# The w2 slabs of the expert stage, begun by ScalarE in a queue of its own

## The chip, the core and the metric

The kernel runs on one core of a Trainium2 chip. The metric is the device time of one launch in microseconds (us). The time before is the median of three runs.

## The reference, cut to what matters

The network has two blocks; the second has two layers, and each of these ends in a mixture of experts. 256 tokens of width 1024 are routed, each to the best two of eight experts in the best of four groups. Each of the 32 experts has three matrices of 2 MB in float32: w1 and w3 (1024 x 512) and w2 (512 x 1024).

```
def expert_block(args):
    tok_b, w_b, e = args
    xb = t[tok_b]
    hid = jax.nn.silu(xb @ w1[e]) * (xb @ w3[e])
    return (hid @ w2[e]) * w_b[:, None].astype(t.dtype)
```

## The kernel before, in words

The program is written out by hand for each engine, with semaphores in between. An expert stage (`moe0`, `moe1`) works through 16 pairs of experts, numbered 0 to 15, 64 token places for each expert. TensorE (`moe_pe`) runs this for pair i: `inner(i, "exp_w1")`, `inner(i, "exp_w3")`, some transposes and the gather of pair i + 1's tokens, and `outer(i)`, which multiplies by w2. After outer(i) comes inner(i + 1, "exp_w1"). Each `inner` or `outer` takes two slabs, one for each expert of the pair, and waits until both have landed. After the inner of pairs 3, 7 and 11 with w1 a few products for the next group of experts come in between; in pairs 4, 8 and 12 a scatter stands ahead of outer.

All weights come through eleven places of 2 MB in SBUF, taken in turn (`Places`, named ring, arena and XTGB in the trace). Slab n takes the place of slab n - 11 and must wait until TensorE has used that one (`free`). SyncE (`moe_sp`) begins every slab, in the order in which TensorE uses them: w1, w1, w3, w3, w2, w2 of pair 0, then of pair 1, and so on. One queue holds them all, so they also land in that order. The slabs of w3 and w2 of pair 15 come in halves.

ScalarE (`moe_act`) applies silu to what w1 gave, copies the transposed hidden values (`x_ht`), and then writes the gathered tokens of pair i + 1 (`turned_x`, eight ACTIVATE of 128x128). Those eight are done when outer(i) has just begun.

Of the kernel before, what the change touches and what calls it, by code (L numbers as in the profile page):

```python
# [12 lines left out]
P = 128  # L13
# [4 lines left out]
SLAB = 4096  # L18
# [6 lines left out]
class Board:  # L25
# [14 lines left out]
    def at(self, *key):  # L40
        if self.counting:
            return []
        return self.known[key]
# [139 lines left out]
def build(nc, d, out, consts):  # L183
    with ExitStack() as ctx:
        board = Board()
        at = board.at
# [32 lines left out]
        sems = {}  # L219
        for name in ("x0", "x1", "aq0", "aq1", "aq2", "aq3", "ident", "rope", "consts", "c", "pos", "gb", "sink", "maska", "ssmp", "late", "keep", "half0", "half1", "half2", "half3", "ada_b", "cols", "mod", "gate_b",  # L220
                     "fox_fb", "mla_g", "abias", "router_b", "rw", "dmask", "srow", "se0", "se1", "se2", "out"):
            sems[name] = ctx.enter_context(nc.semaphore("s_" + name))
        for i in range(NRING + 7):
            sems[f"ring{i}"] = ctx.enter_context(nc.semaphore(f"s_ring{i}"))
        for e in ("pe", "act", "dve", "pool"):
            for st in STAGES:
# [4 lines left out]
        for l in range(2):  # L231
            for j in range(3):
# [5 lines left out]
        ring = Places(slots + [None, None, XTGB] + [arena.ap[:, TOP + j * SLAB:TOP + (j + 1) * SLAB] for j in range(3)]  # L238
                      + [arena.ap[:, 0:SLAB]])
        ring.begin(NRING)  # L240
        shape = {}

        def load(sp, key, src, kc, n, hold=False):
            i, was = ring.take(key, hold)
# [29 lines left out]
        def load_behind_halves(sp, keys, name, offs, kc, n):  # L274

            place = {}
            for h in range(2):
                for key, off in zip(keys, offs):
                    if h == 0:
                        place[key] = ring.take(key)  # L280
                        shape[key] = (kc, n)
                    i, was = place[key]
                    sp.wait_ge(at("free" if h else "free half", was))
                    f = slice(h * SLAB // 2, (h + 1) * SLAB // 2)
                    src = d[name][off:off + P * SLAB].rearrange("(p f) -> p f", p=P)
                    sp.landed(sp.e.dma_start(ring.bufs[i][:, f], src[:, f]), f"ring{i}", ("w", key))
# [1559 lines left out]
        NP = NE // 2  # L1846
# [675 lines left out]
        def mix_dve(v, l, nn):  # L2522
# [11 lines left out]
            k = None  # L2534
            v.wait_ge(at("rope2"))
            for t in range(2):
                if t:
                    x_sums(v, l, nn)
                    for part in range(3):
                        slab_sums(v, l, 0, part)  # L2540
                v.wait_ge(at("rqk", l, t), k)
                k = rope(v, ps_of("rqk", l, t).rearrange("p (h x) -> p h x", h=8), 8, ctab[:, t * 64:t * 64 + 64],
                         stab[:, t * 64:t * 64 + 64], [rqk[:, t, :].rearrange("p (h x) -> p h x", h=8)], rtmp,
                         [("read", "rqk", l, t)], [("rqk rope", l, t)])
# [13 lines left out]
            slab_results(v, l, 1, 2)  # L2558
            slab_sums(v, l, 2, 2)
            slab_results(v, l, 1, 3)  # L2560
            v.wait_ge(at("dmask", l))
            for h in range(4):
                v.wait_ge(at("rs", l, h))
                if h >= 2:
# [7 lines left out]
            for q in range(8):  # L2572
                k = v.then_inc(v.e.bn_stats(st8[:, q, :], ps_of("ro", l, q // 4)[:, (q % 4) * P:(q % 4 + 1) * P]))
                v.wait_ge(k)
                k = v.then_inc(v.e.bn_aggr(mv8[:, q, :], st8[:, q, :]))
# [3 lines left out]
            for t in range(2):  # L2579
                for h in range(4):  # L2580
                    q = t * 4 + h
                    k = v.then_inc(v.ts(rqk[:, t, h * P:(h + 1) * P], ps_of("ro", l, t)[:, h * P:(h + 1) * P],
                                        mv8[:, q, 0:1], rs8[:, q:q + 1], ALU.subtract, ALU.mult), ("read", "ro", l, t))
# [18 lines left out]
            k = v.then_inc(v.tt(lf, misc[:, :, 0:4], fbb.unsqueeze(1).to_broadcast([P, 2, 4]), ALU.add))  # L2602
            v.wait_ge(k)
            k = v.then_inc(v.ts(lt_, lf, -1.0, None, ALU.mult))
# [39 lines left out]
            k = None  # L2644
            for t in range(2):
                kv = kpt[:, t, :].rearrange("p (c x) -> p c x", c=2)
                v.wait_ge(k)
                k = rope(v, misc[:, t, 388:452].unsqueeze(1), 1, ctab[:, t * 64:t * 64 + 64],
                         stab[:, t * 64:t * 64 + 64], [kv[:, 0:1, :], kv[:, 1:2, :]], mtmp, [], [("kp rope", l, t)])
            for t in range(2):  # L2650
                v.wait_ge(at("qp", l, t), k)
                k = rope(v, ps_of("qp", l, t)[:, 0:T].rearrange("p (h x) -> p h x", h=4), 4, ctab[:, t * 64:t * 64 + 64],
                         stab[:, t * 64:t * 64 + 64], [qpt[:, t, :].rearrange("p (h x) -> p h x", h=4)], mtmp,
                         [("read", "qp", l, t)], [])
                v.wait_ge(k)
                k = v.then_inc(v.ts(qpt[:, t, :], qpt[:, t, :], MS, None, ALU.mult), ("qp rope", l, t))
# [40 lines left out]
            k = v.then_inc(v.stt(g, g, 1.0, rgain[:, l, :], ALU.add, ALU.mult))  # L2697
# [294 lines left out]
        def moe_sp(sp, l):  # L2992
            for j, until in ((5, "gate row"), (2, "router")):
                ring.tenant[NRING + j] = (until, l)
                ring.turn.append(NRING + j)
            ring.turn.append(NRING + 6)
            for i in range(NP):
                if i == 2:
                    reg = flag_reg(sp, l)
                offs = [(l * NE + 2 * i + j) * P * SLAB for j in range(2)]  # L3000
                for k, nm in enumerate(("exp_w1", "exp_w3", "exp_w2")):
                    keys = [(nm, l, i, j) for j in range(2)]
                    kc, n = ((8, 512), (8, 512), (4, 1024))[k]
                    if all(ring.tenant[s] in HALVED[l] for s in ring.turn[0:2]):
                        load_behind_halves(sp, keys, nm, offs, kc, n)
                    elif k and i == NP - 1:
                        slabs_in_halves(sp, keys, nm, offs, kc, n, k == 1, 2 * (k == 1))
                    else:
                        for key, off in zip(keys, offs):
                            if key == ("exp_w1", l, 0, 0):  # L3010
                                continue
                            if ring.tenant[ring.turn[0]] in HALVED[l]:
                                load_behind_halves(sp, [key], nm, [off], kc, n)
                            else:
                                slab(sp, key, nm, off, kc, n)
            general(sp, l, reg, general_sp)
            last_over_gate[l] = ring.tenant[NRING + 5]
            last_over_mask[l] = ring.tenant[NRING + 6]
            ring.turn = [i for i in ring.turn if i < NRING]
# [211 lines left out]

        def moe_act(act, l, nn):
            act.stage(f"moe{l}")
            def turned_x(i):
                for c0 in (0, 4) if i else (0, 2, 4, 6):
                    act.wait_ge(at("xg", l, i, c0))
                    if i >= 1:
                        act.wait_ge(at("exp_w3", l, i - 1))
                    for c in range(c0, c0 + (4 if i else 2)):
                        ins = act.act(xg[:, c, :], ps_of("xg", l, i, c0)[:, (c - c0) * P:(c - c0 + 1) * P],  # L3240
                                      ACT.Identity, scale=mcol[l][:, 4, c:c + 1], bias=mcol[l][:, 3, c:c + 1])
                    act.then_inc(ins, ("xg ready", l, i, c0), ("read", "xg", l, i, c0))

            def group_rows(g):
                for n in range(2):
                    act.wait_ge(at("xr", l, g, n))
                    if g:
                        act.wait_ge(at("xg", l, 4 * g - 1, 4))
                    act.then_inc(act.cp(xr_q[:, :, n * 64:(n + 1) * 64],
                                        ps_of("xr", l, g, n).rearrange("p (q c) -> p c q", c=8)), ("xr ready", l, g, n),  # L3250
                                 ("read", "xr", l, g, n))

            group_rows(0)
            turned_x(0)
            act.wait_ge(at("ex", l))
            act.then_inc(act.act(ex, ex, ACT.Exp), ("exp ex", l))
            for i in range(NP):
                act.wait_ge(at("exp_w1", l, i))
                if i >= 1:
                    act.wait_ge(at("xht", l, i - 1))  # L3260
                act.then_inc(act.act(x_s, ps_of("exp_w1", l, i), ACT.Silu), ("silu", l, i),
                             ("read", "exp_w1", l, i))
                if i % 4 == 3 and i + 1 < NP:
                    group_rows(i // 4 + 1)
                act.wait_ge(at("xht", l, i))
                if i >= 1:
                    act.wait_ge(at("xy", l, i - 1, 1))
                act.then_inc(act.cp(x_ht, ps_of("xht", l, i).rearrange("p (a b) -> p a b", a=4)),
                             ("xht ready", l, i), ("read", "xht", l, i))
                if i + 1 < NP:  # L3270
                    turned_x(i + 1)
                if i == 1:
                    reg = flag_reg(act, l)
            general(act, l, reg, general_act)
            if l == 0:
                square_act(act, nn, 0, hrows, X, *av_done(l, 0))
                rms_rows(act, nn, 0, hrows, X, 4, 8)
                square_act(act, nn, 1, hrows, X, *av_done(l, 1))
                for t in range(2):
                    rms_turned_act(act, 1, nn, t)  # L3280
# [460 lines left out]
```

## Time and profile before

| | us |
|---|---|
| median of 3 runs (2283.49 to 2285.26) | 2283.55 |
| the profiled execution, its own time | 2283.03 |
| its span in the profile | 2281.2 |
| TensorE busy | 2249.4 |
| VectorE busy | 1057.5 |
| ScalarE busy | 461.1 |

The profile shows one execution. Busy time is the union of an engine's instructions; a wait stands in square brackets behind the instruction that ended it, with what released it. The span begins with the first instruction and ends with the last. The expert stages lie at about 1100 to 1545 us and 1830 to 2275 us.

### The profile page before, as it was taken

To read this page: it belongs to the slowest core of one execution; us is meant where nothing else is said; L and a number is where in the kernel's file an instruction comes from. 1 tells how busy PE (TensorE), PEld (TensorE's weight loads), DVE (VectorE), ACT (ScalarE), POOL (GpSimd) and SP (SyncE) were. 2 spreads that over 40 slices of the span, in tenths; PEclk is the share of its full clock that TensorE was granted. 3 is DMA by queue.
4 is the path that set the end of the run, shared out by engine and by line. 5 is a ranking of instruction groups with operands and counts; after the bars stand their busy time and mean duration, and the time that the engine had idled before them with its cause. 6 is when DMAs were issued, how large, how long until landed. Compare 5 with 4: busy or idle time off the path is not lost.

```text
span 2281.2 us, 26770 instructions
## 1 busy us (share of the span) xinstructions
PE 2249.4 (99%) x11302; PEld 1377.5 (60%) x11302; DVE 1057.5 (46%) x2098; ACT 461.1 (20%) x1041; POOL 74.4 (3%) x131
## 2 busy tenths in 40 slices
PE   9999999999999999999999999999999999999998
PEld 6569547886497459997533433335999743333343
DVE  4578756668588567675311111125767421111122
ACT  3411003358111011230211111101122021111111
POOL 2000000010000000000000000000000000000000
PEclk9999999999999999999999999999999999999999
DMA  7378725354689515246999999995424899999997
GB/s 296 116 313 358 309 76 202 149 184 162 246 346 407 181 54 211 98 185 256 410 427 428 428 427 427 427 419 210 175 78 168 344 426 427 427 427 428 427 427 285
DMA packets 59318, 672.52 MB, mean 295 GB/s; under 512 B 7521, under 2 KB 7809, under 8 KB 18865
## 3 DMA queue, kind: packets, MB, share of 16 engines
q1 hardware_dynamic: 51888, 649.45, 69.2%
q0 software_dynamic: 7296, 21.21, 2.7%
q8 instruction: 93, 1.52, 0.3%
q14 instruction: 41, 0.33, 0.0%
HBM read 667.37 MB, written 3.26 MB: 294 GB/s over the span
## 4 chain that ended last, share of the span: by engine, by line
PE 89%; DMA 7%; DVE 3%; issue 0%; POOL 0%; ACT 0%; SPq 0%; DVEq 0%; POOLq 0%; ACTq 0%
PE ps L101 86%; DMA ring<-in_exp_w 5%; DVE arena L114 1%; DVE arena L117 1%; PE ps L350 1%; DMA arena<-ssm_rows 1%; PE ps L3112 1%; DMA ring<-in_ada_w 0%; PE ps L639 0%; DMA ring<-in_attn_w_in 0%; PE ps L2139 0%; DVE X L117 0%; DVE arena L110 0%; PE ps L1328 0%; POOL small L117 0%
## 5 line engine op out<-in xcount | busy, mean ns | idle before, releaser
L101 PE MATMUL ps<-arena 128*64 128x512 f32 (+5 forms) x4612 | 1075.9, 446 | 12.6 <-DVE arena L117 4.6
L101 PEld LDWEIGHTS ps<-arena 128*128 128x128 f32 (+2 forms) x4612 | 536.5, 168 | 425.3 <-issue 393.5
L101 PE MATMUL ps<-ring,arena 128*64 128x512 f32 (+2 forms) x1592 | 501.8, 583 | 1.5 <-DMA ring<-in_exp_w 1.5
L101 PE MATMUL ps<-XTGB,ring 128*128 128x256 f32 (+1 forms) x2032 | 382.5, 344 | 0.0
L101 PEld LDWEIGHTS ps<-XTGB,ring 128*128 128x128 f32 x2032 | 333.5, 191 | 43.8 <-issue 9.5
L101 PEld LDWEIGHTS ps<-ring,arena 128*64 128x64 f32 (+1 forms) x1592 | 185.0, 151 | 240.7 <-issue 236.4
L122 DVE COPY arena<-ps 128x512 f32<-128x512 f32 (+5 forms) x133 | 63.3, 496 | 401.1 <-PE ps L101 282.3
L121 ACT COPY arena<-ps 128x512 f32<-128x512 f32 (+3 forms) x187 | 85.0, 473 | 690.2 <-PE ps L101 283.6
L117 DVE TENSOR_TENSOR arena<-ps,arena 128x256 f32<-128x256 f32 (+5 forms) x290 | 127.1, 475 | 119.1 <-PE ps L101 89.0
L101 PE MATMUL ps<-XTGB,arena 128*128 128x128 f32 (+2 forms) x736 | 178.4, 396 | 0.0
L101 PE MATMUL ps<-ring,XTGB 128*128 128x512 f32 (+3 forms) x484 | 166.4, 498 | 1.9 <-DMA ring<-in_attn_w_in 1.8
L117 DVE TENSOR_TENSOR arena<-arena,ps 128x512 f32<-128x512 f32 x36 | 24.7, 687 | 291.7 <-PE ps L101 291.7
L105 ACT ACTIVATE arena<-ps 128x512 f32<-128x512 f32 (+2 forms) x83 | 44.2, 536 | 554.8 <-PE ps L101 549.9
L105 ACT ACTIVATE arena<-arena 128x256 f32<-128x256 f32 (+4 forms) x235 | 119.3, 549 | 146.8 <-DVE arena L117 113.5
L117 DVE TENSOR_TENSOR arena<-arena 128x256 f32<-128x256 f32 (+7 forms) x272 | 127.2, 489 | 21.3 <-PE ps L101 11.0
L101 PEld LDWEIGHTS ps<-ring,XTGB 128*128 128x128 f32 x484 | 89.0, 191 | 70.8 <-issue 61.5
L101 PE MATMUL ps<-arena,ring 128*128 128x128 f32 (+1 forms) x960 | 131.3, 289 | 0.0
L101 PEld LDWEIGHTS ps<-arena,ring 128*128 128x128 f32 x960 | 122.2, 192 | 3.2
L101 PEld LDWEIGHTS ps<-XTGB,arena 128*128 128x128 f32 (+1 forms) x736 | 94.9, 173 | 39.7 <-issue 37.7
L114 DVE SCALAR_TENSOR_TENSOR arena<-arena 128x256 f32<-128x256 f32 (+3 forms) x224 | 94.2, 442 | 50.7 <-ACT arena L105 23.2
L114 DVE SCALAR_TENSOR_TENSOR arena<-ring,small,arena 128x512 f32<-128x512 f32 x140 | 105.3, 752 | 5.0
L105 ACT ACTIVATE arena<-ps,small 128x128 f32<-128x128 f32 (+1 forms) x264 | 96.8, 471 | 37.8 <-PE ps L101 37.7
(162 smaller groups left out, 1050.6 us busy)
## 6 DMA issues: line engine op xcount, KB each, us to landing
arena<-in_exp_w SPq DMA_DIRECT2D x96, 2048.0 KB, 28.9
ring<-in_exp_w SPq DMA_DIRECT2D x64, 2048.0 KB, 28.0
ring<-in_mlp_w SPq DMA_DIRECT2D x25, 2048.0 KB, 11.4
ring<-in_ada_w SPq DMA_DIRECT2D x20, 2048.0 KB, 9.5
XTGB<-in_exp_w SPq DMA_DIRECT2D x16, 2048.0 KB, 28.5
ring<-in_ssm_w_in SPq DMA_DIRECT2D x12, 2048.0 KB, 8.2
ring<-in_w_in SPq DMA_DIRECT2D x12, 2048.0 KB, 8.0
ring<-in_gate_w SPq DMA_DIRECT2D x12, 2048.0 KB, 7.9
```

Source lines behind the costliest of these rows:

```text
L101: return self.e.matmul(o, lhsT=lhsT, rhs=rhs, start=start, stop=stop, skip_group_check=True)
L105: return self.e.activation(o, i, func, bias=bias, scale=scale)
L114: return self.e.scalar_tensor_tensor(out=o, in0=i0, scalar=s, in1=i1, op0=op0, op1=op1)
L117: return self.e.tensor_tensor(o, a, b, op)
L121: return self.e.copy(o, i)
L122: return self.e.tensor_copy(o, i)
L350: ins = pe.e.transpose(ps[:, j * P:(j + 1) * P], i, C["ident"][0:m, 0:m])
L3112: ins = pe.e.transpose(ps[:, f * P:(f + 1) * P], x_h[:, f:512:4], C["ident"])
```

## The change

ScalarE begins the w2 slabs of pairs 2 to 13, in both expert stages: 12 pairs, two slabs each, two stages, 48 transfers. SyncE only books their places, so that every slab keeps the place that it had. ScalarE begins the two slabs of pair i + 1 in its turn i, right behind `turned_x(i + 1)`. They have semaphores of their own. Pairs 0, 1, 14 and 15 stay as they were. One wait is added on VectorE in the mixer, for a constant that landed much earlier.

```diff
--- before.py
+++ after.py
@@ -221,6 +221,7 @@
                      "fox_fb", "mla_g", "abias", "router_b", "rw", "dmask", "srow", "se0", "se1", "se2", "out"):
             sems[name] = ctx.enter_context(nc.semaphore("s_" + name))
         for i in range(NRING + 7):
+            sems[f"ringa{i}"] = ctx.enter_context(nc.semaphore(f"s_ringa{i}"))
             sems[f"ring{i}"] = ctx.enter_context(nc.semaphore(f"s_ring{i}"))
         for e in ("pe", "act", "dve", "pool"):
             for st in STAGES:
@@ -238,7 +239,7 @@
         ring = Places(slots + [None, None, XTGB] + [arena.ap[:, TOP + j * SLAB:TOP + (j + 1) * SLAB] for j in range(3)]
                       + [arena.ap[:, 0:SLAB]])
         ring.begin(NRING)
-        shape = {}
+        shape, place_of = {}, {}
 
         def load(sp, key, src, kc, n, hold=False):
             i, was = ring.take(key, hold)
@@ -2558,7 +2559,7 @@
             slab_results(v, l, 1, 2)
             slab_sums(v, l, 2, 2)
             slab_results(v, l, 1, 3)
-            v.wait_ge(at("dmask", l))
+            v.wait_ge(at("late"), at("dmask", l))
             for h in range(4):
                 v.wait_ge(at("rs", l, h))
                 if h >= 2:
@@ -3003,6 +3004,10 @@
                     kc, n = ((8, 512), (8, 512), (4, 1024))[k]
                     if all(ring.tenant[s] in HALVED[l] for s in ring.turn[0:2]):
                         load_behind_halves(sp, keys, nm, offs, kc, n)
+                    elif k == 2 and 2 <= i < NP - 2:
+                        for key, off in zip(keys, offs):
+                            place_of[key] = (*ring.take(key), off)
+                            shape[key] = (kc, n)
                     elif k and i == NP - 1:
                         slabs_in_halves(sp, keys, nm, offs, kc, n, k == 1, 2 * (k == 1))
                     else:
@@ -3231,6 +3236,15 @@
 
         def moe_act(act, l, nn):
             act.stage(f"moe{l}")
+
+            def load_w2(i):
+                for j in range(2):
+                    key = ("exp_w2", l, i, j)
+                    s, was, off = place_of[key]
+                    act.wait_ge(at("free", was))
+                    act.landed(act.e.dma_start(ring.bufs[s], d["exp_w2"][off:off + P * SLAB].rearrange("(p f) -> p f", p=P)),
+                               f"ringa{s}", ("w", key))
+
             def turned_x(i):
                 for c0 in (0, 4) if i else (0, 2, 4, 6):
                     act.wait_ge(at("xg", l, i, c0))
@@ -3269,6 +3283,8 @@
                              ("xht ready", l, i), ("read", "xht", l, i))
                 if i + 1 < NP:
                     turned_x(i + 1)
+                if 2 <= i + 1 < NP - 2:
+                    load_w2(i + 1)
                 if i == 1:
                     reg = flag_reg(act, l)
             general(act, l, reg, general_act)
```

On SyncE, the end of an expert stage before: the slabs of pairs 12, 13 and 14, each row one matrix of a pair or a part of one (`in_exp_w1` is expert matrix w1).

```order
L248 DMA arena<-in_exp_w1 128x4096 x2
L248 DMA arena<-in_exp_w3 128x4096 x2
L248 DMA XTGB<-in_exp_w2 128x4096
L248 DMA arena<-in_exp_w2 128x4096
L248 DMA ring<-in_exp_w1 128x4096 x2
L248 DMA ring<-in_exp_w3 128x4096 x2
L248 DMA arena<-in_exp_w2 128x4096 x2
L248 DMA arena<-in_exp_w1 128x4096 x2
L248 DMA arena<-in_exp_w3 128x4096
L248 DMA XTGB<-in_exp_w3 128x4096
L248 DMA arena<-in_exp_w2 128x4096
L248 DMA ring<-in_exp_w2 128x4096
```

The same place in the changed program:

```order
L249 DMA arena<-in_exp_w1 128x4096 x2
L249 DMA arena<-in_exp_w3 128x4096 x2
L249 DMA ring<-in_exp_w1 128x4096 x2
L249 DMA ring<-in_exp_w3 128x4096 x2
L249 DMA arena<-in_exp_w1 128x4096 x2
L249 DMA arena<-in_exp_w3 128x4096
L249 DMA XTGB<-in_exp_w3 128x4096
L249 DMA arena<-in_exp_w2 128x4096
L249 DMA ring<-in_exp_w2 128x4096
```

The w2 rows of pairs 12 and 13 have left SyncE's queue; those of pair 14 are still there.

On ScalarE before, around its turn 12: the tokens of pair 13 (two rows of four ACTIVATE), then silu and the copy of the hidden values of pair 13, then the tokens of pair 14.

```order
L105 ACTIVATE arena<-ps0,small 128x128 x4
L105 ACTIVATE arena<-ps1,small 128x128 x4
L105 ACTIVATE arena<-ps3 128x512
L121 COPY arena<-ps0 128x512
L105 ACTIVATE arena<-ps1,small 128x128 x4
L105 ACTIVATE arena<-ps7,small 128x128 x4
```

The same place in the changed program:

```order
L105 ACTIVATE arena<-ps0,small 128x128 x4
L105 ACTIVATE arena<-ps1,small 128x128 x4
L3245 DMA arena<-in_exp_w2 128x4096 x2
L105 ACTIVATE arena<-ps3 128x512
L121 COPY arena<-ps0 128x512
L105 ACTIVATE arena<-ps1,small 128x128 x4
L105 ACTIVATE arena<-ps7,small 128x128 x4
```

The two transfers of pair 13's w2 now stand behind the tokens of pair 13 and ahead of its silu.

## Rows read from the trace of the kernel before

**Rows 1.** The page: busy time of the engines, DMA share in 40 slices.

```profile
PE 2249.4 (99%) x11302; PEld 1377.5 (60%) x11302; DVE 1057.5 (46%) x2098; ACT 461.1 (20%) x1041; POOL 74.4 (3%) x131
...
DMA  7378725354689515246999999995424899999997
```

**Rows 2.** Stretches: length, busy time of each engine, granted clock, DMA share, GB/s.

```profile
1184.00:1435.00 251.00, 250.03 (x1163) 98.88 (x1159) 36.93 (x79) 40.93 (x97) 0.00 (x0) 1.00 1.01 427
1435.00:1465.00 30.00, 29.13 (x131) 11.85 (x131) 6.89 (x12) 3.84 (x10) 0.00 (x0) 1.00 1.01 428
```

**Rows 3.** TensorE's timeline, first stage: start, us, instruction, wait before it.

```profile
1408.63 7.09 PE L101 MATMUL ps<-ring,arena 128*64 128x512 f32 x32
...
1435.84 8.14 PE L101 MATMUL ps<-arena 128*64 128x512 f32 x34 [1.82 <-DMA arena<-in_exp_w]
...
1465.20 1.08 PE L101 MATMUL ps<-ring,arena 128*64 128x512 f32 x4 [0.23 <-DMA ring<-in_exp_w]
...
1484.74 0.65 PE L101 MATMUL ps<-arena 128*64 128x512 f32 x2 [0.75 <-issue]
```

**Rows 4.** Chain that ended last, first stage: start, us, what.

```profile
1354.34 8.07 PE ps L101 x34
...
1390.84 25.94 PE ps L101 x110
...
1427.20 37.87 DMA ring<-in_exp_w
```

**Rows 5.** TensorE's timeline, the same four places of the second stage.

```profile
2163.35 1.08 PE L101 MATMUL ps<-arena 128*64 128x512 f32 x4 [1.76 <-DMA arena<-in_exp_w]
...
2192.71 0.65 PE L101 MATMUL ps<-ring,arena 128*64 128x512 f32 x2 [0.23 <-DMA ring<-in_exp_w]
...
2212.24 0.65 PE L101 MATMUL ps<-arena 128*64 128x512 f32 x2 [0.74 <-issue]
...
2242.93 1.51 PE L101 MATMUL ps<-ring,arena 128*64 128x512 f32 x6 [1.03 <-DMA ring<-in_exp_w]
```

**Rows 6.** ScalarE's timeline, first stage.

```profile
1335.69 2.91 ACT L105 ACTIVATE arena<-ps,small 128x128 f32<-128x128 f32 x8 [1.17 <-PE ps L101]
...
1364.76 2.91 ACT L105 ACTIVATE arena<-ps,small 128x128 f32<-128x128 f32 x8 [1.17 <-PE ps L101]
1379.65 0.60 ACT L105 ACTIVATE arena<-ps 128x512 f32<-128x512 f32 x1 [11.99 <-PE ps L101]
...
1389.87 2.90 ACT L105 ACTIVATE arena<-ps,small 128x128 f32<-128x128 f32 x8 [1.17 <-PE ps L101]
...
1419.18 2.90 ACT L105 ACTIVATE arena<-ps,small 128x128 f32<-128x128 f32 x8 [1.17 <-PE ps L101]
...
1446.32 2.91 ACT L105 ACTIVATE arena<-ps,small 128x128 f32<-128x128 f32 x8 [1.17 <-PE ps L101]
```

**Rows 7.** DMA queues at 1101 to 1113: packets, MB, share of 16 engines.

```profile
q1 hardware_dynamic: 265, 3.98, 78.0%
q0 software_dynamic: 250, 1.02, 20.9%
```

**Rows 8.** Single transfers: out_w, then the expert slabs begun at 1442 to 1444.

```profile
DMA to landing us min/median/max: 7.7/10.1/12.4
...
L248 SPq DMA_DIRECT2D arena<-in_exp_w x2: 328/380/433, 1443.0 to 1443.3; - x2
...
DMA to landing us min/median/max: 41.7/43.9/46.2
```

**Rows 9.** SyncE's timeline: the slabs begun there.

```profile
1442.96 0.80 SPq L248 DMA_DIRECT2D arena<-in_exp_w  x2
...
1523.59 4.92 SPq L248 DMA_DIRECT2D ring<-in_w_in  x4
```

**Rows 10.** TensorE's longest wait, and the stretch behind it (columns of rows 2).

```profile
1548.63 1.86 PE L350 MATMUL ps<-c_ident,arena 128*128 128x128 f32 x8 [4.09 <-issue]
...
1549.00:1552.00 3.00, 2.87 (x9) 1.93 (x9) 1.43 (x5) 1.51 (x4) 0.00 (x0) 0.50 0.69 295
```

## The prediction

> **What bounds the kernel now.** I read the page first. TensorE is busy for 99% of the span, and the DMA engines are at nine tenths in two long blocks, the expert stages [rows 1]. Then the stretches: from 1184 to 1435 us TensorE is busy for 250 of 251 us at the full granted clock (1.00, the 2.4 GHz level), and the DMA engines are at 1.01 of their time with 427 GB/s [rows 2]. Both limits bind. Which ends last is told by TensorE's own waits. In the first stage it waits 1.82 us for w3 of pair 12, 0.23 for w3 of pair 13 and 0.75 for w1 of pair 14 [rows 3], 2.8 us in all; in the second 1.76, 0.23, 0.74 and 1.03 for w1 of pair 15 [rows 5], 3.8 in all. So both stages start with weights well ahead; the transfers lose ground pair by pair, because a pair's six slabs need 6 x 4.9 = 29.4 us and TensorE's pair needs about 25 to 29; and the two meet at pair 12. The chain says the same: 37.87 us from begin to landing at 1427.20 + 37.87 = 1465.07, the one long DMA piece of this stage [rows 4].
>
> One number rests on this: the slab period. W3 of pair 12 landed at 1435.84 - 0.14 = 1435.70 (0.14 being what lies between the landing at 1465.07 and the start at 1465.20), w3 of pair 13 at 1465.07, six slabs later: 4.895 us each, which is also 2.097 MB at 427 GB/s. W3 of pairs 9, 10, 11 therefore landed at 1347.5, 1376.9, 1406.3.
>
> **The change part by part.** *No bytes go away.* The DMA engines move the same slabs at a full 427 GB/s, and 1.01 leaves nothing for a second queue to fill. What changes is the order in which bytes arrive.
>
> *How two queues share.* The trace of before has one overlap, where GpSimd's queue ran beside SyncE's: from 1101 to 1113 us the two moved 250 and 265 packets, in all 5.0 MB in 12 us, 417 GB/s [rows 7]. Packet for packet, at no gain in rate. There the packets were of 4 and 15 KB, so the bytes went 1.0 to 4.0. Here both queues carry the same slabs of equal rows, so I take half each: 9.8 us per slab instead of 4.9 for as long as both have work. The Trainium skill, "DMA: Bandwidth & Descriptors", section "Queues, rings and completion order", says that each DMA engine goes round robin between queues at packet granularity. The row agrees (250 to 265).
>
> *What is late next.* ScalarE begins w2 of pair i when its eight ACTIVATE end. That was at T = 1338.6, 1367.7, 1392.8, 1422.1, 1449.2 for pairs 9 to 13 [rows 6]. SyncE's queue is deep then (41.7 to 46.2 us from begin to landing at the end [rows 8], eight to nine slabs), and w3 of the same pair is not in yet. Before, w2 stood behind w3. Now it takes half the rate away from it. If w3 would have landed at F and the second queue moves bytes from A on, w3 lands at F + (F - A), at most 9.8 us late. A is T plus a start. A slab alone took 7.7 us [rows 8] against 4.9 of transfer, so start and end cost 2.8 us; the start is between 0 and 2.8, and I take half, 1.5. TensorE is ready for w3 at N = 1354.3 and 1379.65 [rows 4, 6], 1408.6, 1435.84 - 1.82 = 1434.0 and 1465.20 - 0.23 = 1465.0 [rows 3]. With S the delay so far:
>
> Pair 9: A 1340.1, F - A = 7.4, lands 1354.9, ready 1354.3; wait 0.6, S 0.6.
> Pair 10: A 1369.2 + 0.6 = 1369.8; 7.1; lands 1384.0, ready 1380.2; wait 3.8, S 4.4.
> Pair 11: A 1394.3 + 4.4 = 1398.7; 7.6; lands 1413.9, ready 1413.0; wait 0.9, S 5.3.
> Pair 12: A 1423.6 + 5.3 = 1428.9; 6.8; lands 1442.5, ready 1439.3; wait 3.2, S 8.5. Of this 1.8 was there before, so 6.7 is new.
> Pair 13: A 1450.7 + 6.7 = 1457.4; 7.7; lands 1472.8, ready 1471.7; wait 1.1. TensorE starts at 1472.9 where it started at 1465.2: 7.7 us later.
>
> Pairs 8 and earlier had more margin: N - F falls from pair to pair, 6.8 at pair 9, 2.75 at pair 10. The series corrects itself: a later TensorE begins w2 later, so less is taken from w3. With a start of 0 it ends at 9.2 instead of 7.7, with 2.8 at 7.1; the hard limit is 9.8.
>
> *What absorbs it.* W1 of pair 14 lands at 1484.6 as before, because the same bytes stand ahead of it. The 0.75 us wait is swallowed: first stage + 7.7 - 0.75 = 6.9. Behind it SyncE's next loads, the four w_in slabs from 1523.59 on [rows 9], are begun when TensorE frees places, so they and the next mixer move along. In the second stage the landings for w1 of pairs 14 and 15 swallow 0.74 and 1.03: + 5.9. Together 12.9 us.
>
> *Is w2 itself in time?* It needs 19.6 us at half rate and up to 2.8 around that: T + 22.4 = 1390.1 for pair 10, and outer(10) began at 1390.84 [rows 4]. 0.7 us to spare. If that fails by a little, a wait at outer takes the place of a wait at w3 and the end hardly moves, by the same self-correction.
>
> *Small parts.* Beginning a slab takes an engine 328 to 433 ns [rows 8], so 0.8 us per pair on ScalarE, which then is idle for 11.99 us [rows 6]: nothing. If that cover were gone it would be 24 x 0.8 = 19 us. SyncE does less. VectorE's new wait is for a transfer that ended long before: nothing. A second queue may cost something outside the span; what lies there now is 2283.03 - 2281.2 = 1.8 us, and I add nothing.
>
> The sum: 2283.03 + 12.9 = 2295.9. The profiled execution is 0.5 below the median of the runs, so **2296**.
>
> **The rivals.** *One line for both.* If transfers of both engines are served in the order in which they are begun, w2 of pair 13, begun at 1449.2, stands behind the slabs begun at 1442.96 and 1443.3 [rows 9], the last of which lands 46.2 us later [rows 8], at 1489.5. Outer(13) is ready at 1465.2 + 11.2 (the step from 1379.65 to 1390.84) = 1476.4. It waits 13.1, less the absorbed waits: 12.4 + 11.3 = 23.7, so 2307. The alternation in rows 7 speaks against it; that was another kind of queue, though. Chance 0.1.
>
> *ScalarE's queue gets less than half.* Then w2 is late for every pair. At a third it needs 29.4 + 2.8 us of the 25.1 to 29.2 between two outers less 2.0: 5 to 9 us of wait per pair until the slack is gone, somewhere near 24 x 3 = 70 us, 2350. Nothing shows such a split. Chance 0.04.
>
> *TensorE's clock.* After its wait of 4.09 us the granted clock was 0.50 (1.2 GHz) in the next stretch [rows 10]; the wait of 1.82 left it at 1.00 [rows 2]. Mine are up to 3.8. A drop of 3 us costs about 1.5; but ahead of pair 13 it is absorbed like any other delay. At most 2300.
>
> *No change.* The Trainium skill says on the same page, "Issuing engines are not separate DMA queues", that beginning transfers on several engines saves only the time to begin them. By that rule alone the time would stay at 2283.5. As a mechanism here: if w3 landed in time all the same, because ScalarE's first packets come more than 6 us after T, nothing would move. The 7.7 us of a lone slab allow 2.8. Chance 0.08, within 0.2%, which is 4.6 us and about what a measurement of this kernel can tell.
>
> *Faster.* Two queues could lift the rate. To break even w3 of pair 13 must land about 6.5 us sooner; over the 57 slabs between 1184 and 1465 us that is 0.11 us each, 437 instead of 427 GB/s; above that the waits of now go, at most 2.8 + 3.8 us: 2277. The 417 GB/s of rows 7 speak against it. Chance 0.05.
>
> **How the numbers follow.** The half-and-half case has 0.73. With a start of 2.8 us it gives 2 x 7.1 - 2.5 = 11.7, with the hard limit 2 x 9.8 - 2.5 = 17.1; a misreading of N by 1 us per stage widens that, so its own range is 2292 to 2302. With the one-line case it holds 0.83, and part of the second may fall a little outside, so the range is 2288 to 2308. Faster 0.05, same 0.09, slower 0.86.
>
> **What would show it.** Right: TensorE waits of 1 to 4 us on expert slabs from pair 9 or 10 on, at w3 and hardly at outer; w2 from begin to landing about 22 us; DMA share still 1.0 at 427 GB/s; about 7 us more by pair 13, and none in pairs 14 and 15. Waits at outer with w2 taking 40 us: one line. No waits at all and more than 435 GB/s: faster. I am wrong if the split is by something else than packets.

## The result, and the profile after

The changed kernel takes 2302.2 us (median of 6, 2301.35 to 2304.29) against 2283.6 before (6 runs): ratio 1.0081, 95% interval 1.007 to 1.0091. It is slower by 18.6 us. The prediction said slower, 2296, range 2288 to 2308. Its direction, its mechanism and its stated range held. The sum of 12.9 us was too small by 5.7, and the narrower range that it gave for this mechanism alone, 2292 to 2302, was just missed: the stated range reaches 2308 because it also covers the case of one line for both engines, which did not come true.

The page of the changed kernel: TensorE's busy time, and the DMA queues (packets, MB, share of 16 engines).

```profile
PE 2256.8 (98%) x11302; PEld 1378.2 (60%) x11302; DVE 1057.4 (46%) x2098; ACT 460.9 (20%) x1041; POOL 74.4 (3%) x131
...
q1 hardware_dynamic: 44976, 548.78, 58.4%
q10 hardware_dynamic: 6912, 100.67, 10.3%
```

ScalarE's queue is q10, with 48 slabs of 2.1 MB. The bytes in all are as before, but TensorE now has 98% of a longer span. Its timeline shows where, first for the expert stage of layer 0, then of layer 1.

```profile
1358.82 1.98 PE L101 MATMUL ps<-ring,arena 128*64 128x512 f32 x4 [4.08 <-DMA ring<-in_exp_w]
...
1417.86 1.98 PE L101 MATMUL ps<-ring,arena 128*64 128x512 f32 x4 [3.04 <-DMA ring<-in_exp_w]
...
1476.63 1.94 PE L101 MATMUL ps<-ring,arena 128*64 128x512 f32 x8 [1.70 <-DMA ring<-in_exp_w]
...
2096.41 1.12 PE L101 MATMUL ps<-ring,arena 128*64 128x512 f32 x2 [4.28 <-DMA ring<-in_exp_w]
...
2156.31 1.08 PE L101 MATMUL ps<-ring,arena 128*64 128x512 f32 x4 [4.05 <-DMA ring<-in_exp_w]
...
2214.20 1.08 PE L101 MATMUL ps<-ring,arena 128*64 128x512 f32 x4 [1.89 <-DMA ring<-in_exp_w]
```

These are the waits for w3 of pairs 9, 11 and 13 in each stage; the waits of before for w3 of pair 12 and w1 of pairs 14 and 15 [rows 3, 5] are gone. No wait stands at outer, so w2 is in time (19.4 us in the median from begin to landing, 14.1 to 24.9; the prediction had about 22). The two queues share as forecast. Here is the first stage's pair 13, with q10's slabs landing beside SyncE's, from 1461 to 1480 us.

```profile
q1 hardware_dynamic: 281, 4.10, 50.5%
q10 hardware_dynamic: 271, 4.00, 49.7%
```

Two things stand here that the prediction did not have. These are stretches of the changed kernel (length, busy time of each engine, granted clock, DMA share, GB/s):

```profile
1132.00:1152.00 20.00, 20.00 (x99) 8.12 (x97) 1.54 (x4) 4.09 (x10) 0.00 (x0) 1.00 0.93 369
...
1184.00:1435.00 251.00, 243.87 (x1115) 97.07 (x1113) 35.15 (x75) 40.30 (x96) 0.00 (x0) 0.98 1.01 427
1355.00:1365.00 10.00, 6.18 (x22) 2.20 (x24) 0.20 (x1) 0.01 (x1) 0.00 (x0) 0.83 1.02 433
1410.00:1430.00 20.00, 16.96 (x56) 6.50 (x53) 1.45 (x4) 2.35 (x4) 0.00 (x0) 0.83 1.01 430
```

Against the 1184 to 1435 row of [rows 2] TensorE has 6.2 us less. First, in the 20 us from 1132 on, the DMA engines moved only 369 GB/s. The same stretch of the kernel before:

```profile
1132.00:1152.00 20.00, 20.00 (x101) 8.09 (x98) 1.40 (x3) 4.09 (x10) 0.00 (x0) 1.00 1.02 433
```

(433 - 369) GB/s x 20 us = 1.28 MB, which is 3.0 us of DMA time lost for good. The same 20 us of the second stage have 364 against 430 GB/s. Second, the granted clock fell to half behind the longer waits (0.83 in the rows of 1355 and 1410).

To compare the stages of different runs I take times from the end of TensorE's wait just ahead of a stage's work (1099.96 before, 1100.35 after), since what lies ahead of it shifts by some tenths, in some runs by 1 to 2.6 us. Stage 1 ends with the last wait of 0.79 us (1542.55 before, 1553.01 after). Stage 2 lies likewise from 1827.52 to 2271.28 before and from 1837.75 to 2290.58 after. Stage 1 is 10.1 us longer, stage 2 9.1. What lies between them takes 285.0 before and 284.7 after, so nothing there absorbs or adds more than some tenths. (The two stages make 19.2 us, the two profiled spans differ by 19.3, the medians by 18.6.)

### The profile page after: what moved, and what is told of

It is laid out like the page before. It is cut to its first block, busy times and chain, and to the rows that moved or that the text cites. A ratio compares the mean times of both kernels' runs of the same rounds, so it can differ in the third digit from the quotient of the medians.

```text
span 2300.5 us, 26770 instructions
## 1 busy us (share of the span) xinstructions
PE 2256.8 (98%) x11302; PEld 1378.2 (60%) x11302; DVE 1057.4 (46%) x2098; ACT 460.9 (20%) x1041; POOL 74.4 (3%) x131
## 4 chain that ended last, share of the span: by engine, by line
PE 81%; DMA 13%; DVE 5%; issue 0%; ACT 0%; POOL 0%; SPq 0%; DVEq 0%; POOLq 0%; ACTq 0%
PE ps L101 79%; DMA ring<-in_exp_w 10%; DVE arena L114 2%; DVE arena L117 2%; DMA arena<-ssm_rows 1%; PE ps L351 1%; DMA ring<-in_ada_w 1%; PE ps L3117 1%; DMA arena<-in_mlp_w 1%; DVE X L117 0%; DMA ring<-in_attn_w_in 0%; PE ps L640 0%; PE ps L2140 0%; DVE arena L110 0%; ACT arena L106 0%
## 5 line engine op out<-in xcount | busy, mean ns | idle before, releaser
L101 PE MATMUL ps<-ring,arena 128*64 128x512 f32 (+2 forms) x1592 | 509.0, 593 | 19.0 <-DMA ring<-in_exp_w 19.0
L117 DVE TENSOR_TENSOR arena<-arena 128x256 f32<-128x256 f32 (+7 forms) x272 | 127.3, 490 | 20.6 <-PE ps L101 10.9
```

The source lines that it names most:

```text
L101: return self.e.matmul(o, lhsT=lhsT, rhs=rhs, start=start, stop=stop, skip_group_check=True)
L117: return self.e.tensor_tensor(o, a, b, op)
```

## The experiments

Each is timed in rounds beside the kernel before on the same chip. The first four share a median of before of 2284.4, the next four 2283.9, the last three 2283.9.

**One pair alone.**

```diff
-                    elif k == 2 and 2 <= i < NP - 2:
+                    elif k == 2 and 13 <= i < 14:
...
-                if 2 <= i + 1 < NP - 2:
+                if 13 <= i + 1 < 14:
```

> ScalarE begins the w2 slabs of pair 13 alone (both stages); all others stay with SyncE. Theory (order of bytes): w2 of pair 13 takes half the rate from 1451 us on, all of it ahead of w3 of pair 13, which lands 9.8 us late; 9.8 twice less the 2.5 us of waits that are swallowed gives +17.1, and up to 3.4 more if the long wait drops the clock: 2300 to 2304. Rival (every slab in a second queue costs a little, or the queue itself costs): one pair of twelve, 18.6 / 12 = +1.6: 2285. One pair should cost nearly as much as twelve.

Measured: 2303.1 us, ratio 1.008 (1.0063 to 1.0097), + 18.7. One pair costs as much as twelve; an equal share of the cost for each pair is out. That the two agree to 0.1 us is luck, though: this run has no DMA gap and loses more to the clock. TensorE's timeline of this run, w3 of pair 13 in both stages:

```profile
1475.74 1.12 PE L101 MATMUL ps<-ring,arena 128*64 128x512 f32 x2 [6.15 <-DMA ring<-in_exp_w]
...
2213.52 1.12 PE L101 MATMUL ps<-ring,arena 128*64 128x512 f32 x2 [7.86 <-DMA ring<-in_exp_w]
```

The stretch around the first (columns as above, the granted clock third from the end):

```profile
1470.00:1485.00 15.00, 9.26 (x31) 3.19 (x32) 0.06 (x1) 0.00 (x0) 0.00 (x0) 0.77 1.01 429
```

From the stage's first wait (1100.70 in this run) w3 of pair 13 starts at 375.0, before at 365.2: 9.8 us later, the two slabs of w2 to a tenth. The stages end 11.6 and 10.0 us later: 9.8 less the swallowed 0.75 leaves 9.1 for the first, and the half clock behind the long wait makes the rest. TensorE also stood 1.96 us ahead of w1 of pair 13 (to 1460.44), which the kernel before does not. The profile names VectorE there; by the slab period w1 itself landed at about that time, for w2 took half the rate from it too. The wait for w3 absorbed that.

**Pairs 4 to 13.** The same two lines, with `4 <= i < NP - 2`.

> ScalarE begins w2 of pairs 4 to 13; pairs 2 and 3 are back with SyncE. Theory: the changed kernel has a DMA gap at 1144 to 1150 us, about 3 us, because w2 of pair 2 is begun 11 to 18 us later than before while SyncE's queue is short; this moves every later landing by 3.1 us per stage. Without it: 2283.6 + 12.9 = 2296.5, as the prediction's sum had it. Rival (the missing 5.7 us come from the clock, which fell to half for 10 and 7 us): no change from the changed kernel, 2302.

Measured: 2300.3 us, ratio 1.0068 (1.0051 to 1.0085), + 15.9. This is neither the theory's value nor the rival's. The gap is gone, but the waits now lie at pairs 10 and 13 (and 0.55 us at 12), and the one at 13 is long:

```profile
1383.96 1.40 PE L101 MATMUL ps<-arena 128*64 128x512 f32 x4 [4.28 <-DMA arena<-in_exp_w]
...
1474.27 1.12 PE L101 MATMUL ps<-ring,arena 128*64 128x512 f32 x2 [4.30 <-DMA ring<-in_exp_w]
```

The stretch around the second:

```profile
1470.00:1485.00 15.00, 10.73 (x34) 3.44 (x34) 1.05 (x2) 0.25 (x1) 0.00 (x0) 0.77 1.01 431
```

W3 of pair 13 starts 9.0 us late instead of 11.0, which is what the missing gap gave back. The clock behind it takes about 2.6 us, as in the run before (stage 1 is 10.9 us longer = 9.0 - 0.75 + 2.6). The changed kernel had no such loss behind its last wait, so most of what the gap gave back in the first stage went to the clock. Stage 2 is 8.0 us longer, against 9.1.

**Pairs 2 to 11.** The same two lines, with `2 <= i < NP - 4`.

> ScalarE begins w2 of pairs 2 to 11; pairs 12 and 13 are back with SyncE. Theory: w3 of pair 11 is the last one delayed; TensorE is 8.8 us late there, and the waits of now at pairs 12, 13 and 14 (2.8 us, in the second stage 3.8) are swallowed: 6.0 + 5.0 = +11: 2294.6. Rival (each pair costs its share): 10 of 12 pairs, +15.5: 2299.

Measured: 2300.0 us, ratio 1.0066 (1.0049 to 1.0083), + 15.5, the rival's value by the median, and 5 above the theory's. The trace gives another reason: w3 of pair 11 starts 9.6 us late (the theory had 8.8), the wait there is 4.10 us, and the clock falls behind it. Stage 1 is 8.8 us longer: 9.6 less the 2.8 swallowed is 6.8, and 2 are the clock's. Stage 2 is 7.6 longer. By itself this run does not decide; together with the run of pair 13 alone, where the rival says + 1.6, it does.

**Idle products in the waits, first try.** Six products ahead of `inner(i, "exp_w3")` of pairs 9 and 11.

```diff
+                if i in (9, 11):
+                    ps = bank(pe, "fill", l, i)
+                    for _ in range(6):
+                        ins = pe.mm(ps, C["ident"], C["tri"], True, True)
+                    pe.then_inc(ins, ("read", "fill", l, i))
                 inner(i, "exp_w3")
```

> The changed kernel, with six idle products of 128x512 (about 2.7 us) on TensorE ahead of its wait for w3 of pairs 9 and 11, so that the granted clock doesn't fall there. Theory: delays ahead of pair 13 are absorbed, because a later TensorE begins w2 later; the clock stays at 1.00, the waits grow, and the time stays at 2302 within 1.5. Rival (the clock's loss is part of the cost): 10.2 and 6.8 us at half clock come back as 5.1 + 3.4 = 8.5: 2294.

Measured: 2304.5 us, ratio 1.0092 (1.0075 to 1.0108). This is 1 us above what the theory allowed and 10 above the rival, and the run was badly sized. The products' row:

```profile
1413.62 5.40 PE L101 MATMUL ps<-c_tri,c_ident 128*128 128x512 f32 x12
```

Six took 5.4 us (each stands as two records of 0.45), more than the waits of 4.1 and 3.0 that they were to fill, so the clock stayed up and about as much time was spent. The run says nothing alone.

**Pairs 4 to 8.** The two lines with `4 <= i < 9`.

> ScalarE begins w2 of pairs 4 to 8 alone, 5 pairs of 12. Theory (order of bytes counts only where w3 is nearly late): these pairs have over 6.8 us of margin at w3, pair 8 a wait of at most 2 us, which the landings at pairs 12 to 14 swallow: no change, 2284 within 2. Rival (each pair costs its share of 18.6): + 7.8, 2292.

Measured: 2283.0 us, ratio 1.0001 (0.9991 to 1.001). No change: a second queue, ten slabs per stage through it, costs nothing where w3 has margin, to within 0.1%.

**Pairs 2 to 8.** The two lines with `2 <= i < 9`.

> As the run with pairs 4 to 8, with pairs 2 and 3 too. Theory: the only thing added is the DMA gap at 1144 to 1150 us, about 3.1 us per stage; every landing behind it moves by that, and TensorE, which waits for weights at pairs 12 to 14 anyway, ends 3.1 later in each stage: + 6.2, 2290.5. Rival (the gap is early and is made good): no change, 2284.

Measured: 2290.6 us, ratio 1.0029 (1.0018 to 1.0041), + 6.6. The stages are 3.2 and 3.3 longer. The early stretch, first of the run with pairs 2 to 8:

```profile
1132.00:1152.00 20.00, 20.00 (x99) 8.15 (x97) 1.70 (x4) 4.09 (x10) 0.00 (x0) 1.00 0.93 365
```

and of the run with pairs 4 to 8:

```profile
1132.00:1152.00 20.00, 20.00 (x99) 8.13 (x97) 1.41 (x3) 4.09 (x10) 0.00 (x0) 1.00 1.01 427
```

In between lies the whole difference of the two kernels. The DMA gap is early, TensorE waits for nothing in the 250 us behind it, and then the gap is paid in full.

**One queue, other order.** The kernel before, where SyncE begins pairs 3 to 13 as w1, w2, w3.

```diff
+                if 3 <= i < NP - 2:
+                    place = {}
+                    for k, nm in enumerate(("exp_w1", "exp_w3", "exp_w2")):
...
+                            place[key] = (*ring.take(key), off)
...
+                    for nm in ("exp_w1", "exp_w2", "exp_w3"):
+                        for j in range(2):
+                            key = (nm, l, i, j)
+                            s, was, off = place[key]
+                            sp.wait_ge(at("free", was))
```

> The kernel before, with one queue on SyncE for all, in which pairs 3 to 13 are begun in the order w1, w2, w3 (places as before). No second queue. Theory (it is the order of bytes, not the queue): w3 lands 9.8 us late for each of these pairs; TensorE starts w3 of pair 13 9.9 us late, less the swallowed 2.5: + 17.3, 2301, up to 3 more if the clock falls at the last wait. Rival (a second queue costs in itself): no change, 2284.

Measured: 2307.2 us, ratio 1.0104 (1.0087 to 1.012), + 23.3. With no second queue at all it costs more than the change. The theory had + 17.3, at most 3 more. The surplus over 17.3 is seen in the trace: a small DMA gap in each stage, and the clock behind the wait at pair 12, which is the last one here; at pair 13 TensorE is already later than the landing. TensorE's timeline there:

```profile
1447.73 1.72 PE L101 MATMUL ps<-arena 128*64 128x512 f32 x6 [3.99 <-DMA arena<-in_exp_w]
```

Two stretches of this run:

```profile
1160.00:1184.00 24.00, 24.00 (x119) 9.55 (x117) 3.11 (x7) 4.08 (x10) 0.00 (x0) 1.00 0.98 407
1445.00:1455.00 10.00, 7.26 (x26) 2.80 (x28) 0.00 (x0) 0.00 (x0) 0.00 (x0) 0.83 1.00 428
```

The DMA engines moved 407 instead of 427 GB/s for 24 us, which is 1.1 us. The stages are 12.0 and 12.2 us longer.

**Pairs 4 to 13 with idle products, first try.** Seven, five and two products ahead of w3 of pairs 10, 12 and 13.

> ScalarE begins w2 of pairs 4 to 13, and idle products on TensorE fill the greater part of its waits at w3 of pairs 10, 12 and 13, so that the clock stays up. Theory: without the DMA gap and without a clock loss behind the last wait the prediction's own sum is left, + 12.9: 2296.5 to 2297. Rival (the sum of the prediction was too low for another reason): as the run with pairs 4 to 13, 2300.

Measured: 2300.4 us, ratio 1.0073 (1.0056 to 1.009). That is the rival's 2300, but the mistake of size is the same: the products ran 6.3, 4.6 and 1.9 us, and TensorE came to w3 later than it landed. The run decides nothing.

**The changed kernel with fewer idle products.** The block of the first try with 4, 2, 1 and 1 products ahead of w3 of pairs 9 to 12. Pairs 10 and 12 had no wait to fill in the changed kernel, so their three products are added work.

> The changed kernel with 4, 2, 1 and 1 idle products (0.9 us each) on TensorE ahead of w3 of pairs 9 to 12, each time less than the wait there. (The six of the run before took 5.4 us, longer than the waits of 4.1 and 3.0, so it told the clock's part from nothing.) Theory: the clock stays up, the waits at pairs 10 to 13 grow by what the clock no longer takes, TensorE starts w3 of pair 13 about 11 us late as before: 2302. Rival (the clock's loss adds): 8.5 less, 2294.

Measured: 2302.5 us, ratio 1.0079 (1.0063 to 1.0094), as the changed kernel. In stage 1 the clock fell all the same at pair 11. In stage 2 it held from 2090 to 2212 us, where in the changed kernel it had fallen twice:

```profile
2090.00:2212.00 122.00, 119.04 (x536) 47.04 (x532) 16.70 (x35) 17.48 (x42) 0.00 (x0) 1.00 1.01 427
```

There the wait at pair 13 grew from 1.89 to 3.21 us, and w3 of pair 13 started 11.8 late, against 11.3 in the changed kernel:

```profile
2215.66 1.08 PE L101 MATMUL ps<-ring,arena 128*64 128x512 f32 x4 [3.21 <-DMA ring<-in_exp_w]
```

TensorE was ready for it 0.8 us sooner and started no sooner: what is lost or won ahead of the last delayed w3 costs or gives nothing here. Behind this wait of 3.21 us the clock fell, and that was paid: stage 2 is 11.2 us longer, against 9.1 in the changed kernel. (The profiled execution took 2305.5 us, 3 more than the median of the four.)

**Pairs 4 to 13 with fitting idle products.** Four and two products ahead of w3 of pairs 10 and 12.

> ScalarE begins w2 of pairs 4 to 13; 4 and 2 idle products ahead of w3 of pairs 10 and 12, less than the waits there, in place of 7, 5 and 2, which took 6.3, 4.6 and 1.9 us and overran them. Theory: no DMA gap, no clock loss behind the last wait, TensorE 7.7 us late at w3 of pair 13: 2283.9 + 12.9 = 2297. Rival (another loss of 3 to 4 us that the sum lacks): 2300.

Measured: 2295.2 us, ratio 1.0048 (1.0033 to 1.0064), + 11.3. Without the gap and with the clock held, the prediction's own case comes out: + 12.9 lies within the interval of + 7.5 to + 14.6, the rival's + 16 does not. TensorE's timeline at w3 of pairs 12 and 13:

```profile
1441.67 0.65 PE L101 MATMUL ps<-arena 128*64 128x512 f32 x2 [1.61 <-DMA arena<-in_exp_w]
...
1472.45 1.08 PE L101 MATMUL ps<-ring,arena 128*64 128x512 f32 x4 [1.64 <-DMA ring<-in_exp_w]
```

The stretch around the second, at the full clock:

```profile
1470.00:1485.00 15.00, 13.36 (x67) 6.43 (x66) 1.54 (x3) 3.26 (x9) 0.00 (x0) 1.00 1.00 427
```

W3 of pair 13 starts 7.8 us late (the sum had 7.7), stage 1 is 6.8 longer (6.9), stage 2 4.8 (5.9). In stage 2 there is no wait at w3 of pair 13: TensorE, 7.3 us late from pair 12 on, came behind its landing, swallowed the 0.23 us of before, and was 7.0 late instead of 7.7.

**The copy of X left out.** The kernel before, where GpSimd's 1 MB copy is made only if the fallback is needed.

```diff
-            pool.landed(pool.e.dma_start(dkeep[l], X), "keep", ("keep", l))
+            reg = flag_reg(pool, l)
+            with pool.e.If_ne(reg, 0):
+                pool.e.dma_start(dkeep[l], X).then_inc(sems[f"kept{l}"], 16)
+                pool.e.wait_ge(sems[f"kept{l}"], 16)
```

> The kernel before, in which GpSimd writes its 1 MB copy of X (used only if an expert has more tokens than places) after it has read the flag, and only if the flag is set; with these inputs it isn't. Theory (each us of DMA time ahead of pair 12 counts once, up to the waits there): 2.5 us of DMA time less per stage, the waits of 2.8 and 3.8 us shrink by that: - 5.0, 2278.9. Rival (the landings at pairs 12 to 14 don't bind): no change, 2283.9.

Measured: 2284.3 us in 11 runs, ratio 1.0 (0.9991 to 1.0009). There is no gain. The number is the rival's; its reason (the landings at pairs 12 to 14 don't bind) is refuted by the run with pairs 2 to 8. The stretch of this run, then of the kernel before:

```profile
1100.00:1132.00 32.00, 30.25 (x157) 14.08 (x158) 8.68 (x43) 9.47 (x22) 0.86 (x3) 1.00 0.97 392
```

```profile
1100.00:1132.00 32.00, 31.42 (x164) 14.42 (x166) 8.25 (x38) 9.47 (x22) 0.00 (x0) 1.00 1.01 421
```

The DMA engines moved 29 GB/s x 32 us = 0.9 MB less there and stood idle instead: the next slab waits for TensorE to free its place. (The stage begins 2.6 us later in this run; from there on the 32 us give 393 GB/s, and the stages are as long as before to 0.1 us.) So DMA time ahead of 1132 us is not what binds, and my theory was wrong to count from there. Nothing in these runs beats the kernel before.

## Why the prediction held, and where its sum fell short, point by point

**Both limits bind, and the waits at pairs 12 to 14 tell it.** Right. The runs with pairs 2 to 8 and 4 to 8 show it best: 3.0 us of DMA time lost at about 1140 us come out as 3.2 and 3.3 us at the stages' ends.

**Half each, packet for packet.** Right: 281 and 271 packets. The Trainium skill's round robin between queues ("DMA: Bandwidth & Descriptors", "Queues, rings and completion order") agrees with these counts.

**W3 lands at F + (F - A), at most 9.8 late.** Right: 9.8 with pair 13 alone, 7.8 with pairs 4 to 13 and a steady clock. The pairs at which TensorE waits came out differently in the changed kernel: 4.08, 3.04 and 1.70 us at pairs 9, 11 and 13, where the sum had waits of 0.6 to 3.8 at all five from 9 to 13. With the DMA gap the first wait is at pair 9, without it at pair 10. That it is the order of bytes, and not the queue, is shown by the one-queue run (+ 23.3) and the run with pairs 4 to 8 (0).

**A, when the second queue's bytes begin to move.** Right by luck: two errors cancel. I had the transfer begun when the eight ACTIVATE end. ScalarE's timeline of the changed kernel for pair 13:

```profile
1456.28 1.15 ACT L105 ACTIVATE arena<-ps,small 128x128 f32<-128x128 f32 x3 [1.17 <-PE ps L101]
1457.18 0.33 ACTq L3245 DMA_DIRECT2D arena<-in_exp_w  x1
...
1457.55 0.45 ACTq L3245 DMA_DIRECT2D arena<-in_exp_w  x1
1457.67 1.51 ACT L105 ACTIVATE arena<-ps,small 128x128 f32<-128x128 f32 x4
```

ScalarE begins it among them, 2.0 us before the last ends. From 1457 to 1460.6, though, no packet of q10 is seen, only SyncE's:

```profile
q1 hardware_dynamic: 107, 1.57, 102.6%
```

The first comes 3.5 us behind the begin. Less the 2.0 us this is 1.5 us behind the last ACTIVATE, just where the prediction had put it.

**"The DMA engines move the same slabs at a full 427 GB/s".** This is the step that failed. It holds from 1184 us on and not at 1144. Before, w2 of pair 2 was begun as soon as its places were free, at about 1130 and 1137; now ScalarE begins it at 1148.8. SyncE's queue, which got one slab at 1130.3 and one at 1137.2, ran dry. I looked at the depth of the queue at the end of the stage (42 to 46 us) and not at its beginning. The missing term is 3.0 to 3.3 us per stage, measured as + 6.6 by the run with pairs 2 to 8; 12.9 + 6.6 = 19.5 against 18.6. The prediction put this term at nothing.

**"The series corrects itself".** Only half right. Let c be the F - A of pair 13 without any delay, 1465.1 - 1450.7 = 14.4 us. Each us of delay S that TensorE brings to pair 13 begins w2 later and takes as much off the landing of w3, so its start is late by the larger of S and c - S, and by 9.8 at most. That is least where the two meet, at c / 2 = 7.2 us without the gap. In three runs without the gap S was 6.4, 4.9 and 0; the rule gives 8.0, 9.5 and 9.8, and 7.8, 9.0 and 9.8 were measured. So where the waits fall decides up to 2.6 us per stage, and the sum's 7.7 was near the least that it could be.

**The clock.** Right that its loss ahead of pair 13 is absorbed (the changed kernel with fewer products, stage 2). What I passed over is a fall behind the last wait, which nothing absorbs: 2.6 us in stage 1 of the run with pairs 4 to 13. The changed kernel itself escaped it, with last waits of 1.70 and 1.89.

**The rivals.** One line for both would have shown waits at outer; there are none. Less than half for ScalarE's queue is ruled out by 281 to 271 packets. No change, and faster: the rate stayed at 427 GB/s. That agrees with the Trainium skill's "Issuing engines are not separate DMA queues" (same page), by which all transfers run on the same DMA engines whoever begins them. But the order alone moved the time, which that rule does not speak of. The swallowed waits were as forecast.

In the run with fitting products stage 2 came out 1.1 us shorter than the sum. Of this 0.7 is the missing wait at its pair 13, told there; the rest stays open.

## What to carry to other kernels

Where transfers and compute tie, a queue's order is its schedule. A second queue with slabs of the same kind gave its bytes half the rate at once, and what was needed sooner landed later by what passed it. Ask of each moved transfer when it was begun before, how full the queue was then, at the start of a stage as well as at its end, and which slab now stands behind it. A cost that one moved transfer shows as fully as twelve is set where the last delayed load meets the compute, not by adding up transfers. DMA time saved ahead of a wait for places was worth nothing here.

## What the runs showed of the hardware that was not expected

ScalarE began a transfer while ACTIVATE written ahead of it were still running, 2.0 us before the last of them ended. The first packet of the second queue came 3.4 to 3.6 us after the begin in all 24 pairs of slabs, beside a busy first queue; before, at 1048.14 us, SyncE's first came 1.0 us after the begin, with nothing else to move. Whether the engine or the busy queue makes the difference is not shown. A slab alone took 7.7 us from begin to landing where 4.9 are transfer. Waits of 3.04, 4.08 and 4.28 us on TensorE were each followed by a stretch at half the granted clock (1.2 GHz), waits of 1.70 and 1.82 by none. Between them it is not settled by length: 2.75 us (pairs 2 to 8, stage 1) and 3.23 us (first try with idle products) were followed by none either, while 2.75 us in stage 2 of the same run with pairs 2 to 8 and 1.96 us in stage 2 of the run with pairs 4 to 8 were followed by such a stretch. The block of 32 products that takes 7.09 us at 2.4 GHz took 8.8 and 10.0 us behind the two long waits of the run with pairs 4 to 13.
